# RWKV bonus of a hybrid decoder: two multiplications moved to GpSimd, VectorE's sum placed behind its mix

## The chip, the cores and the metric

The kernel runs on one core of a Trainium2 chip, in one launch. The metric is the device time of the whole program in microseconds (us), lower is better; a figure for the kernel is the median of several executions. PE is TensorE, DVE is VectorE, ACT is ScalarE, POOL is GpSimd, SP is SyncE, which issues most transfers.

## The reference, cut to what matters

One step of a decoder with two layers. Each layer projects its input once and splits the result among three branches: an RG-LRU, an RWKV-7 time mixing with 4 heads of 64, and a latent attention over a paged cache. The three results are gated, joined, projected and normalised. This case concerns the RWKV branch. Its rows are 1040 prompt tokens and 8 sequences of 8 new tokens; here is the part that counts:

```python
u_prev = jnp.concatenate([shift_prev[:, None, :].astype(u.dtype), u[:, :-1]], axis=1)
du = u_prev - u
mix = lp['rk_mix']
xr = u + du * mix[0]
xk = u + du * mix[2]
xv = u + du * mix[3]
r = xr @ lp['rk_wr']
...
k_mod = k.astype(F32) * (1.0 + (a - 1.0) * lp['rk_ka'].astype(F32))
...
o = o + jnp.sum(r_h * k_h * lp['rk_rk'].astype(F32), axis=-1, keepdims=True) * v_h
```

The last line is the bonus: for each token and head, the product of r, the modified key and a weight, summed over the head's 64 elements, times v. All arithmetic is float32.

## The kernel before, in words

Each layer is five blocks with a barrier between them: projection, RWKV, prompt attention, sample attention, output. The RWKV block works on 9 tiles of 128 tokens (RT), t = 0 to 8; in the last one the 64 new tokens sit in the lower half. The first tile's projections, mix and decayed keys are made at the end of the projection block already, beside TensorE's large products; so is the mix of tile 1.

For each tile the block solves a small triangular system, in nine stages by the names prod, n2, z1, z2, z3, mid, zf, wu, wt (SOLVE). This is a chain: TensorE multiplies 32x32 pieces, ScalarE or VectorE takes the result out of PSUM, VectorE transposes or adds, TensorE goes on. Beside each stage the engines do other work on neighbouring tiles, written down in the table BESIDE: for a stage, (work, distance in tiles, piece). From it comes one list, RWKV_ORDER. Every engine walks through the same list and runs the pieces it has a function for (run), so the table sets each engine's order, and semaphores alone tie the engines together. At the stage wt of tile t there stand `("bonus", 1, 0)`, the bonus of tile t + 1, and `("mix", 2, 0)`, the mix of tile t + 2. Before the first tile the list FRONT runs flip and bonus of tile 0.

The pieces that matter, by VectorE's lines in this kernel:
- unit and keys_decay (L1419 to L1437): the last of the new keys. The product L1434 releases s_keys and writes btkt, L1437 writes bk. Both read bbkm, whose half bbkm[:, 1] is the modified key.
- write (L1534, two instructions): updates the running state from PSUM.
- bonus_: rk = r times modified key (L1440), rk = rk times weight (L1441), sums by head into sc4 (L1444), which releases s_bon.
- mix: du (L1386) and six scalar_tensor_tensor (L1391), which release s_mix.
- prod: masks the two PSUM banks of TensorE's stage prod (L1454, L1459), then a transpose and an add (L1463, L1464).

On TensorE, prod (L1064) follows the transposes of flip (L1052), which wait for s_keys, and ScalarE's copy of them (L1291). After prod come low, one read (L1170, L1173) and the first projection of the next tile (L1019). That projection waits for the mix (s_mix) and for VectorE's mask L1459 (s_x), and the stage n2 of the solve stands behind it in TensorE's order. ScalarE, after the copies of flip, scales v by the sums (bonus_, L1298, waits s_bon), then takes out low (L1247, L1248) and the projection (L1255).

GpSimd has little to do in this block: a power of a 128x4 tile twice a tile, as tensor_tensor with ALU.pow (L973 for the key norms, L977 for the group norm), and in the last tile a memset and a product (L982, L990).

Of the kernel before, what the change touches and what calls it, by code (L numbers as in the profile page):

```python
# [18 lines left out]
ALU = mybir.AluOpType  # L19
# [246 lines left out]
def project_block(nc, m):  # L266
# [488 lines left out]
    "mid": [("write", -1, 2), ("gate", -2, 0)],  # L755
    "zf": [("read", -1, 3), ("unit", 1, 0), ("keys_decay", 1, 0)],
    "wu": [("write", -1, 3), ("out", -1, 0), ("flip", 1, 0)],
    "wt": [("bonus", 1, 0), ("mix", 2, 0)]}
FRONT = [("flip", 0), ("bonus", 0)]
RWKV_ORDER = [(f, 0, k) for f, k in FRONT]  # L760
BACK = [("read", 1, 0), ("norm", 0, 0), ("read", 1, 1), ("centre", 0, 0), ("out", 1, 0), ("finish", 0, 0),
# [8 lines left out]
def rwkv_weights(m):  # L770

    w = Memory()
    w.rkw, w.w1, w.w2 = carve(m.work[:, X_AT + DK * T:], (2, 3, WA), (2, 2 * LORA), (2, WA))
    w.prow, w.s_in = carve(m.work[:, W_AT[1] + 8 * Z_COLS - 8 * Z_AT[Z_LOADS[-2]]:W_AT[0]], (7, WA), (NB, 2, HD))
    return w
# [16 lines left out]
def rwkv_block(nc, m):  # L792
# [5 lines left out]
    sem, layer, const = m.sem, m.layer, m.const  # L798
# [8 lines left out]
    s_rkve = sem("s_rkve")  # L807
# [9 lines left out]
    s_keys = sem("s_keys")  # L817
# [3 lines left out]
    s_bon = sem("s_bon")  # L821
# [23 lines left out]
    s_dve = sem("s_dve2")  # L845
    s_sto = sem("s_sto2")
    s_pl = sem("s_pl")
    s_um = sem("s_um")
    rw = rwkv_weights(m)
    rkw, w1, w2, prow, s_in = rw.rkw, rw.w1, rw.w2, rw.prow, rw.s_in  # L850
    fw = rwkv_front(m)
    wl, xm, tw, r_sb, k_sb, v_sb, wa, sg, logd, dec, kk, sqj, ss, bbkm, na, btkt, rt, pc, bk, du = \
# [42 lines left out]
    def heads(x):  # L895
        return x.rearrange("p (h j) -> p h j", h=H_B)
# [12 lines left out]
    def prm(n):  # L909
        return prow[:, n, :]  # L910
# [21 lines left out]
    def steps_to(t):  # L932
        return sum(len(steps(i)) for i in range(t))
# [9 lines left out]
    def of_each(x):  # L943
        return x.rearrange("p (o n) -> p o n", o=1).to_broadcast([NS, SEQ_CH, WA])

    def run(stages):

        for stage, t, k in RWKV_ORDER:
            if stage in stages:
                stages[stage](t, k)  # L950

    N_LD = 16 * 6
    with nc.Block() as block:
        @block.sync
        def _(sp):
            pw = prompt_weights(m)
            for k in range(2):
                sp.dma_start(pw.wuq[:, k], m.wuq[layer, :, k].rearrange("p (h n) -> p h n", h=H_C)).then_inc(m.s_wq, 16)
            sp.dma_start(pw.wuk, m.wuk[layer]).then_inc(m.s_wk, 16)
            sp.dma_start(pw.wuv, m.wuv[layer]).then_inc(m.s_wuv, 16)  # L960
            sp.dma_start(tail, m.consts[:, C_N:]).then_inc(m.s_wuv, 16)
            sp.wait_ge(s_state, steps_to(RT) + 1)
            sp.dma_start(m.o_wkv[layer], s_out).then_inc(s_sto, 16)

            sp.wait_ge(s_sto, 16)

        @block.gpsimd
        def _(pool):
            half = const[:, C_EPS + 1:C_EPS + 2].to_broadcast([P, H_B])

            def keys_norm(t, _):
                pool.wait_ge(s_ss, t + 1)
                nc.gpsimd.tensor_tensor(ss[:, 1, :], ss[:, 0, :], half, ALU.pow).then_inc(s_rn, 1)  # L973

            def norm(t, _):
                pool.wait_ge(s_var, t + 1)
                nc.gpsimd.tensor_tensor(mv[:, :, 3], mv[:, :, 2], half, ALU.pow).then_inc(s_gr, 1)  # L977

            def clear(t, _):
                if t == LAST_T:  # L980
                    pool.wait_ge(s_rkv, 3 * RT)
                    nc.gpsimd.memset(flat_m, 0.0).then_inc(s_pl, 1)  # L982
                    pool.wait_ge(s_pl, 1)

            def split_values(t, _):
                if t == LAST_T:
                    pool.wait_ge(m.s_wuv, 32)
                    pool.wait_ge(s_rkve, 3 * RT)
                    pool.wait_ge(s_rd, 2 * steps_to(LAST_T))
                    nc.gpsimd.tensor_tensor(vm[SMP], of_each(v_sb[SMP, t % 3, :]), own_rows, ALU.mult).then_inc(s_pl, 1)  # L990
                    pool.wait_ge(s_pl, 2)

            run({"keys_norm": keys_norm, "norm": norm, "sums": clear, "wt": split_values})

        @block.tensor
        def _(pe):
            bank = m.bank

            def low(t, _):
                pe.wait_ge(s_fold, 1)  # L1000
                if t >= 1:
                    pe.wait_ge(s_fle, 2 * t)
                for n in range(2):
                    for k in range(2):
                        last = nc.tensor.matmul(bank[7][0:2 * LORA, 0:P], wl[:, n, k, :],
                                                prev_of(t, k) if n else m.ub[:, k, 1 + t * P:1 + (t + 1) * P],
                                                start=n == 0 and k == 0, stop=n == 1 and k == 1)
                last.then_inc(s_lo1, 1)
# [13 lines left out]
            def lora(t, _):  # L1022
                pe.wait_ge(s_lo1e, t + 1)
                for i in range(2):
                    last = nc.tensor.matmul(bank[7][:, i * WA:(i + 1) * WA], tw[0:LORA + 1, i, :], w2[0:LORA + 1, i, :],
                                            start=True, stop=True)
                last.then_inc(s_lo2, 1)

            def sums(t, _):
                pe.wait_ge(s_sg, t + 1)  # L1030
                pe.wait_ge(s_rkve, 3 * t + 3)

                if t == LAST_T:
                    pe.wait_ge(m.s_wuv, 32)
                for i, c in enumerate(sums_of(t)):
                    nc.tensor.matmul(bank[2 + i // 2][:, (i % 2) * WA:(i % 2 + 1) * WA], c, logd,
                                     start=True, stop=True)

                each = tail[:, L_TOT:L_N] if t == LAST_T else sqc(C_B32)[:, 0:P:CH]
                n = 1 + NB if t == LAST_T else C4  # L1040
                for k in range(2):
                    last = nc.tensor.matmul(bank[3][:, WA + n * k:WA + n * k + n], logd[:, k * P:(k + 1) * P],
                                            each, start=True, stop=True)
                last.then_inc(s_cum, 1)
# [314 lines left out]
        def _(dve):  # L1359
# [3 lines left out]
            def link(ins):  # L1363

                chain[0] += 1
                ins.then_inc(s_dve, 1)
                dve.wait_ge(s_dve, chain[0])
# [69 lines left out]
                nc.vector.tensor_tensor(bk[:, t % 3], bbkm, twice(dec[:, 3]), ALU.mult).then_inc(s_hat, 1)  # L1437

            def bonus_(t, _):
                link(nc.vector.tensor_tensor(rk, r_sb, bbkm[:, 1], ALU.mult))  # L1440
                link(nc.vector.tensor_tensor(rk, rk, prm(4), ALU.mult))  # L1441
                if t >= 1:
                    dve.wait_ge(s_bv, t)
                nc.vector.tensor_reduce(sc4, heads(rk), AX, ALU.add).then_inc(s_bon, 1)  # L1444
# [118 lines left out]
            def gate(t, _):  # L1563
                dve.wait_ge(s_of, t + 1)
                for k in range(2):
# [10 lines left out]
            nc.vector.tensor_copy(gnb, bank[4][:, 0:2 * P:P])  # L1576
            run({"mix": mix, "decay": decay, "keys_norm": keys_norm, "unit": unit, "keys_decay": keys_decay,
                 "bonus": bonus_, "prod": prod, "n2": squares, "z1": z1, "z2": z2, "z3": z3, "zf": zf, "read": read,
                 "write": write, "norm": norm, "centre": centre, "finish": finish, "gate": gate})

# [938 lines left out]


BLOCKS = [project_block, rwkv_block, prompt_block, sample_block, output_block]


# [101 lines left out]
```

## Time and profile before

| | us |
|---|---|
| median of 3 runs | 2117.56 |
| lowest and highest | 2106.84, 2118.98 |
| profiled execution, its own time | 2116.25 |
| span of its trace | 2114.5 |
| PE busy in the span | 1966.7 (93%) |
| DVE busy | 1027.3 (49%) |
| ACT busy | 646.4 (31%) |
| POOL busy | 223.1 (11%) |
| RWKV block of layer 0 | about 279 to 490 |
| RWKV block of layer 1 | about 1340 to 1550 |

The trace gives for each engine the instructions in order of time. A start is in us from the span's beginning; what stands in square brackets behind a row is how long the engine had been idle and which instruction's end released it. Equal instructions in a row are merged, with a count. Instructions of VectorE overlap a little: the next starts some 0.08 us before the end of the one ahead unless it waits for it. A matmul's end is modelled.

### The profile page before, as it was taken

To read this page: it belongs to the slowest core of one execution; us is meant where nothing else is said; L and a number is where in the kernel's file an instruction comes from. 1 tells how busy PE (TensorE), PEld (TensorE's weight loads), DVE (VectorE), ACT (ScalarE), POOL (GpSimd) and SP (SyncE) were. 2 spreads that over 40 slices of the span, in tenths; PEclk is the share of its full clock that TensorE was granted. 3 is DMA by queue.
4 is the path that set the end of the run, shared out by engine and by line. 5 is a ranking of instruction groups with operands and counts; after the bars stand their busy time and mean duration, and the time that the engine had idled before them with its cause. 6 is when DMAs were issued, how large, how long until landed. Compare 5 with 4: busy or idle time off the path is not lost. (4 is left out here: it accounts for less than half of the span.)

```text
span 2114.5 us, 51148 instructions
## 1 busy us (share of the span) xinstructions
PE 1966.7 (93%) x22506; PEld 1272.1 (60%) x22506; DVE 1027.3 (49%) x2393; ACT 646.4 (31%) x1719; POOL 223.1 (11%) x223
## 2 busy tenths in 40 slices
PE   8999989988899999999989999899888999999997
PEld 5665667774566567654456656677745665677543
DVE  2017137764565458723330171377745664588333
ACT  1222234442554432210012221344434553323100
POOL 0000000110000034202100000011100000342022
PEclk9999999998999989999999999999989999899999
DMA  5102010000001267721121020100000002577221
GB/s 209 50 1 89 1 48 4 4 4 22 1 1 24 67 232 272 258 110 60 66 62 50 1 89 1 47 4 4 4 22 1 1 13 78 222 271 262 73 80 53
DMA packets 50113, 151.14 MB, mean 71 GB/s; under 512 B 15138, under 2 KB 19490, under 8 KB 40420
## 3 DMA queue, kind: packets, MB, share of 16 engines
q1 hardware_dynamic: 37604, 72.36, 10.3%
q0 software_dynamic: 12288, 75.51, 9.6%
q8 instruction: 179, 2.93, 0.6%
q14 instruction: 42, 0.34, 0.1%
HBM read 130.27 MB, written 12.86 MB: 68 GB/s over the span
## 5 line engine op out<-in xcount | busy, mean ns | idle before, releaser
L405 PE MATMUL psum<-work 128*128 128x368 f32 x1536 | 485.7, 477 | 8.8 <-DMA work<-w_z 6.5
L405 PEld LDWEIGHTS psum<-work 128*128 128x128 f32 x1536 | 294.0, 192 | 194.3 <-issue 9.3
L2458 PE MATMUL psum<-work,mixed 128*128 128x512 f32 (+1 forms) x576 | 250.6, 596 | 1.6 <-PEq L2130 1.6
L2458 PEld LDWEIGHTS psum<-work,mixed 128*128 128x128 f32 (+1 forms) x576 | 106.9, 187 | 138.8 <-issue 138.8
L2326 DVE STREAM_TRANSPOSE work<-work 128x1024 f32<-128x1024 f32 x128 | 150.5, 1214 | 0.7 <-issue 0.5
L1902 ACT ACTIVATE work<-psum,work 128x128 f32<-128x128 f32 (+8 forms) x130 | 97.9, 753 | 162.0 <-DVE work L2005 161.5
L1786 PE MATMUL psum<-work 96*128 96x512 f32 (+3 forms) x384 | 140.0, 499 | 3.7 <-ACT work L1902 2.1
L2070 POOL DMA_INDIRECT work<-cache_ckv,pages x64 | 60.7, 948 | 640.1 <-PE psum L1736 397.4
L2230 PE MATMUL psum<-work,ckv 128*64 128x256 f32 x1024 | 118.4, 382 | 1.9 <-issue 1.2
L1786 PEld LDWEIGHTS psum<-work 96*128 96x128 f32 x384 | 68.3, 192 | 62.5 <-issue 46.0
L2506 DVE SCALAR_TENSOR_TENSOR work<-work,psum 128x512 f32<-128x512 f32 (+1 forms) x36 | 23.1, 684 | 163.9 <-PE psum L2458 163.9
L2004 DVE TENSOR_REDUCE work<-psum 128x1 f32<-128x128 f32 (+8 forms) x130 | 99.5, 765 | 4.4
L2230 PEld LDWEIGHTS psum<-work,ckv 128*64 128x64 f32 x1024 | 73.6, 137 | 42.9 <-issue 13.0
L650 DVE TENSOR_TENSOR mixed<-work 128x1104 f32<-128x1104 f32 x4 | 5.2, 1309 | 193.6 <-ACT work L578 193.5
L1797 PE MATMUL psum<-const_sb,work 128*128 128x128 f32 x594 | 88.7, 285 | 10.1 <-ACT work L1911 9.9
L1911 ACT COPY work<-psum 128x512 f32<-128x512 f32 (+1 forms) x166 | 84.3, 545 | 34.3 <-PE psum L1797 33.6
L1797 PEld LDWEIGHTS psum<-const_sb,work 128*128 128x128 f32 x594 | 69.7, 145 | 37.7 <-issue 19.6
L1729 PE MATMUL psum<-cq,work 128*128 128x368 f32 x192 | 74.3, 520 | 19.1 <-DVE work L1960 16.9
L2003 DVE TENSOR_TENSOR psum<-psum,const_sb 128x128 f32<-128x128 f32 (+1 forms) x130 | 38.2, 294 | 101.5 <-PE psum L1786 87.0
L1815 PE MATMUL psum<-work 128*64 128x128 f32 x1152 | 82.7, 282 | 0.0
L2275 ACT ACTIVATE work<-psum,work 128x1024 f32<-128x1024 f32 x32 | 35.7, 1115 | 132.0 <-DVE work L2337 132.0
L522 ACT ACTIVATE mixed<-psum 128x368 f32<-128x368 f32 x48 | 19.4, 477 | 184.9 <-PE psum L405 184.9
(314 smaller groups left out, 2988.2 us busy)
## 6 DMA issues: line engine op xcount, KB each, us to landing
work<-w_z SPq DMA_DIRECT2D x4, 2560.0 KB, 11.2
work<-w_out SPq DMA_DIRECT2D x4, 2048.0 KB, 9.0
xres<-work SPq DMA_DIRECT2D x16, 512.0 KB, 2.9
work<-xT SPq DMA_DIRECT2D x4, 1104.0 KB, 8.9
work<-x_tok SPq DMA_DIRECT2D x8, 512.0 KB, 3.9
work<-xres SPq DMA_DIRECT2D x8, 512.0 KB, 4.3
work<-w_z SPq DMA_DIRECT2D x1, 2304.0 KB, 12.5
o_ckv<-ckv SPq DMA_DIRECT2D x2, 1104.0 KB, 4.3
```

The costliest lines, as they stand in the source:

```text
L405: return nc.tensor.matmul(zb[i % 2][n][:, 0:G], z_weights(m, g)[:, k, lo:lo + Z_W[i]], xT[:, k, span(n)], start=k == 0, stop=k == DK - 1)
L1729: last = nc.tensor.matmul(bank_of(j)[:, 0:G], wuq[:, k, h, :], cq[:, k, span(g)], start=k == 0, stop=k == 1)
L1786: last = nc.tensor.matmul(m.bank[2 * u + b][:, 0:w], qt[0:96, p % 2, u, t * P:(t + 1) * P], kt[0:96, p % 2, u, a:a + w], start=True, stop= ...
L1797: last = nc.tensor.transpose(m.bank[4 + at % 2][0:w, n * P:(n + 1) * P], pr[:, i % 2, u * N_FULL * P + c * P:u * N_FULL * P + c * P + w], ...
L1815: last = nc.tensor.matmul(m.bank[6][u * VD:(u + 1) * VD, 0:P], val[:, c, (2 * p + u) * VD:(2 * p + u + 1) * VD], pT[:, i % 2, n * P:(n + 1 ...
L1902: nc.scalar.activation(pr[:, i % 2, u * N_FULL * P:u * N_FULL * P + keys(i)], scores_of(i, u), ACT.Exp, bias=mx[:, 2 * (i % 2) + u:2 * (i ...
L1911: nc.scalar.copy(pT[0:w, i % 2, 4 * g * P:(4 * g + len(c)) * P], m.bank[4 + at % 2][0:w, 0:len(c) * P]).then_inc(s_pte, 1)
L2004: link(nc.vector.tensor_reduce(sm, scores_of(i, u), AX, ALU.max))
L2070: pool.indirect_dma_start(rows[n % RING][:, s, :], None, m.cache_ckv, row).then_inc(m.s_pg[n % RING], 16)
L2230: last = nc.tensor.matmul(m.bank[6 + n % 2][64 * s:64 * s + 64, 0:R], pT[:, n % 2, j, 64 * s:64 * s + 64], pgc[n % RING][:, s, j * R:(j + ...
L2326: last = nc.vector.transpose(kt[:, half, s], pgc[n % RING][:, s, :].rearrange("p (j k n) -> p j k n", j=KEYS, k=2) [:, :, half, :])
L2458: last = nc.tensor.matmul(yb[t % 2][half][0:n, :], m.mixed[:, k, lo:lo + n], wo[half][:, k, :], start=k == 0, stop=k == DK - 1)
```

## The change

The two multiplications of the bonus leave VectorE. GpSimd gets a function bonus_ that waits for s_keys (the modified keys), for r (s_rkve) and for the previous tile's sums (s_bon), multiplies r by the key, waits for that on its new semaphore s_rk, and multiplies by the weight. VectorE's bonus_ waits for both on s_rk and does the sums. In the table, mix stands ahead of bonus at the stage wt; that moves the sums behind the mix on VectorE, for every tile that has one. ScalarE's scaling of v stays where it was, as it has no mix. FRONT is as it was, so tile 0's products run on GpSimd too.

```diff
-    "wt": [("bonus", 1, 0), ("mix", 2, 0)]}
+    "wt": [("mix", 2, 0), ("bonus", 1, 0)]}
...
+    s_rk = sem("s_rk")
...
-            run({"keys_norm": keys_norm, "norm": norm, "sums": clear, "wt": split_values})
+            def bonus_(t, _):
+                pool.wait_ge(s_keys, t + 1)
+                pool.wait_ge(s_rkve, 3 * t + 2)
+                if t >= 1:
+                    pool.wait_ge(s_bon, t)
+                nc.gpsimd.tensor_tensor(rk, r_sb, bbkm[:, 1], ALU.mult).then_inc(s_rk, 1)
+                pool.wait_ge(s_rk, 2 * t + 1)
+                nc.gpsimd.tensor_tensor(rk, rk, prm(4), ALU.mult).then_inc(s_rk, 1)
+
+            run({"keys_norm": keys_norm, "norm": norm, "sums": clear, "wt": split_values, "bonus": bonus_})
...
             def bonus_(t, _):
-                link(nc.vector.tensor_tensor(rk, r_sb, bbkm[:, 1], ALU.mult))
-                link(nc.vector.tensor_tensor(rk, rk, prm(4), ALU.mult))
+                dve.wait_ge(s_rk, 2 * t + 2)
                 if t >= 1:
                     dve.wait_ge(s_bv, t)
                 nc.vector.tensor_reduce(sc4, heads(rk), AX, ALU.add).then_inc(s_bon, 1)
```

VectorE's queue at the end of a tile, in the middle of the block, before the change. From the last keys (L1434, L1437) over the state update (L1534) and the bonus to the mix and the masks; the names in brackets are the semaphores waited for, s_pe_prod being TensorE's stage prod:

```order
L1434 TENSOR_TENSOR work<-work 128x512 [waits s_dve2]
L1437 TENSOR_TENSOR work<-work 128x512 [waits s_wr]
L1534 SCALAR_TENSOR_TENSOR work<-work,psum 128x64 [waits s_wr]
L1534 SCALAR_TENSOR_TENSOR work<-work,psum 128x64
L1440 TENSOR_TENSOR work<-work 128x256
L1441 TENSOR_TENSOR work<-work 128x256 [waits s_dve2]
L1444 TENSOR_REDUCE work<-work 128x4 [waits s_bv,s_dve2]
L1386 TENSOR_TENSOR work<-ub 128x256
L1391 SCALAR_TENSOR_TENSOR work<-work,pfs,ub 128x128 [waits s_rkv,s_dve2]
L1391 SCALAR_TENSOR_TENSOR work<-work,pfs,ub 128x128 x5
L1454 TENSOR_TENSOR work<-psum,const_sb 128x512 [waits s_o2,s_pe_prod]
```

The same place in the changed kernel, whose line numbers here are larger by ten and, behind GpSimd's new function and the shorter bonus_, by nine:

```order
L1444 TENSOR_TENSOR work<-work 128x512 [waits s_dve2]
L1447 TENSOR_TENSOR work<-work 128x512 [waits s_wr]
L1543 SCALAR_TENSOR_TENSOR work<-work,psum 128x64 [waits s_wr]
L1543 SCALAR_TENSOR_TENSOR work<-work,psum 128x64
L1396 TENSOR_TENSOR work<-ub 128x256
L1401 SCALAR_TENSOR_TENSOR work<-work,pfs,ub 128x128 [waits s_rkv,s_dve2]
L1401 SCALAR_TENSOR_TENSOR work<-work,pfs,ub 128x128 x5
L1453 TENSOR_REDUCE work<-work 128x4 [waits s_bv,s_rk]
L1463 TENSOR_TENSOR work<-psum,const_sb 128x512 [waits s_o2,s_pe_prod]
```

Two rows are gone, the six products and du have moved up to the state update, and the sums stand directly ahead of the mask, with a wait for GpSimd.

GpSimd's queue in the changed kernel, over two tiles in the middle of the block (L974 and L978 are the powers, L973 and L977 before):

```order
L974 TENSOR_TENSOR work<-work,const_sb 128x4 [waits s_ss]
L999 TENSOR_TENSOR work<-work 128x256 [waits s_bon,s_rkve,s_keys]
L1001 TENSOR_TENSOR work<-work 128x256 [waits s_rk]
L978 TENSOR_TENSOR work<-work,const_sb 128x4 [waits s_var2]
L974 TENSOR_TENSOR work<-work,const_sb 128x4 [waits s_ss]
```

The two products are new between the power for the key norm and the one for the group norm; the other three rows stood there one behind the other.

## Rows read from the trace of the kernel before

**Rows 1.** Windows: us, busy us of each engine, PE clock, DMA share, GB/s.
```profile
core 0: us, PE busy (x) PEld busy (x) DVE busy (x) ACT busy (x) POOL busy (x), PEclk, DMA share, GB/s
...
345.00:367.00 22.00, 20.21 (x640) 16.33 (x623) 16.69 (x60) 10.62 (x38) 2.18 (x2) 1.00 0.02 4
```

**Rows 2.** Timeline, DVE, end of a tile: start, us, engine line operation.
```profile
363.79 0.69 DVE L1434 TENSOR_TENSOR work<-work 128x512 f32<-128x512 f32 x1
364.39 0.69 DVE L1437 TENSOR_TENSOR work<-work 128x512 f32<-128x512 f32 x1
365.11 0.47 DVE L1534 SCALAR_TENSOR_TENSOR work<-work,psum 128x64 f32<-128x64 f32 x2
365.50 0.42 DVE L1440 TENSOR_TENSOR work<-work 128x256 f32<-128x256 f32 x1
365.95 0.42 DVE L1441 TENSOR_TENSOR work<-work 128x256 f32<-128x256 f32 x1
366.41 0.42 DVE L1444 TENSOR_REDUCE work<-work 128x4 f32<-128x256 f32 x1
366.75 0.42 DVE L1386 TENSOR_TENSOR work<-ub 128x256 f32<-128x256 f32 x1
367.20 1.67 DVE L1391 SCALAR_TENSOR_TENSOR work<-work,pfs,ub 128x128 f32<-128x128 f32 x6
368.78 0.69 DVE L1454 TENSOR_TENSOR work<-psum,const_sb 128x512 f32<-128x512 f32 x1
```

**Rows 3.** Timeline, PE, the same place: stage prod, the read, the projection.
```profile
366.35 0.86 PE L1064 MATMUL psum<-work 64*32 64x64 f32 x64 [0.51 <-ACT work L1291]
...
368.52 0.30 PE L1173 MATMUL psum<-work 64*32 64x64 f32 x4
369.81 1.10 PE L1019 MATMUL psum<-work 128*128 128x256 f32 x4 [0.99 <-DVE work L1459]
```

**Rows 4.** Line L1454, whole run: both forms, and whom the engine sat idle for.
```profile
L1454 DVE TENSOR_TENSOR work<-psum,const_sb x16: 681/685/693, 282.6 to 1497.3; 128x512 f32<-128x512 f32 x16
L1454 DVE TENSOR_TENSOR work<-psum,work x2: 692/692/692, 457.1 to 1518.4; 128x512 f32<-128x512 f32 x2
...
  PE psum L1064: 3.4, 4
```

**Rows 5.** Timeline, tile 1 of layer 0: PE's stage prod and the mask.
```profile
301.06 1.06 PE L1064 MATMUL psum<-work 64*32 64x64 f32 x64 [0.25 <-ACT work L1291]
...
302.17 0.69 DVE L1454 TENSOR_TENSOR work<-psum,const_sb 128x512 f32<-128x512 f32 x1
```

**Rows 6.** Groups of GpSimd, forms apart: count, busy us, mean ns, idle before.
```profile
L2482 POOL TENSOR_TENSOR work<-work 128x1024 f32<-128x1024 f32 x16 | 37.5, 2343 | 35.0 <-DVE work L2518 35.0
L973 POOL TENSOR_TENSOR work<-work,const_sb 128x4 f32<-128x4 f32 x16 | 18.6, 1160 | 239.3 <-DVE work L1412 239.3
L977 POOL TENSOR_TENSOR work<-work,const_sb 128x4 f32<-128x4 f32 x18 | 18.2, 1009 | 163.8 <-DVE work L1548 163.8
L2479 POOL TENSOR_TENSOR work<-work,const_sb 128x1 f32<-128x1 f32 x16 | 8.8, 553 | 249.0 <-DVE work L2514 249.0
...
L389 POOL COPY ub<-work 128x8 f32<-128x8 f32 x4 | 0.8, 196 | 0.1
```

**Rows 7.** Timeline, where GpSimd's powers meet VectorE's instructions.
```profile
248.72 0.42 DVE L730 SCALAR_TENSOR_TENSOR work<-work 128x256 f32<-128x256 f32 x1
248.96 1.08 POOL L397 TENSOR_TENSOR work<-work,const_sb 128x4 f32<-128x4 f32 x1 [104.24 <-DVE work L729]
...
360.13 0.43 DVE L1414 SCALAR_TENSOR_TENSOR work<-work 128x256 f32<-128x256 f32 x1
360.26 1.17 POOL L973 TENSOR_TENSOR work<-work,const_sb 128x4 f32<-128x4 f32 x1 [9.71 <-DVE work L1412]
360.59 0.47 DVE L1534 SCALAR_TENSOR_TENSOR work<-work,psum 128x64 f32<-128x64 f32 x2
```

**Rows 8.** Timeline, ACT, the same place as rows 2.
```profile
366.87 1.07 ACT L1298 ACTIVATE work<-work 128x64 f32<-128x64 f32 x4 [0.29 <-DVE work L1444]
...
368.55 0.26 ACT L1248 COPY work<-psum 32x128 f32<-32x128 f32 x1
370.95 0.48 ACT L1255 ACTIVATE work<-psum,const_sb 128x256 f32<-128x256 f32 x1 [2.15 <-PE psum L1019]
```

## The prediction, made before the changed kernel was run

> **What bounds the kernel now.** The change touches the RWKV block alone, so I read the windows of that block first. A tile takes 22 us, in which PE is busy for 20.2, DVE for 16.7, ACT for 10.6 and POOL for 2.2, at a granted clock of 1.00, the 2.4 GHz level [rows 1]. PE's share says little: the block is a chain that goes back and forth between engines. What counts is where PE stands still. The largest such place is the first projection of the next tile (L1019): PE's read ends at 368.52 + 0.30 = 368.82, the projection starts at 369.81, and the 0.99 us between are put down to DVE's mask L1459 [rows 3]. The n2 stage of the solve stands behind that projection, so the whole chain waits.
>
> Why is the mask late? DVE's timeline shows it. PE's stage prod, which the mask reads, ends at 366.35 + 0.86 = 367.21 [rows 3], and L1454 starts at 368.78, with no idle time ahead of it: DVE is still in the bonus and the mix [rows 2]. So for 1.57 us DVE's queue is what the chain waits for. Over the run 18 such masks stand, and only 4 of them found DVE idle, 3.4 us together [rows 4]: tiles 0 and 8 of each layer, which have no mix ahead. The other 14 (tiles 1 to 7, two layers) are held by the queue. In tile 1 PE's prod ends at 301.06 + 1.06 = 302.12 and the mask starts at 302.17 [rows 5], so there nearly nothing is to be had.
>
> **What is removed.** L1440 starts at 365.50 and L1444 at 366.41 [rows 2]: the two products and their waits take 0.91 us of DVE's queue. PE can use all of it, since its gap is 0.99. In 12 tiles (2 to 7, twice) a mask 0.91 us earlier makes the chain 0.91 us shorter. The end of the mask's wait for prod would be 1.57 away, so it isn't reached.
>
> **What is added.** GpSimd gets two products of 128x256. No row has that form. Its 128x1024 add takes 2.34 us; a copy of 128x8, nearly all fixed cost, 0.196; a power of one element per partition 0.55 [rows 6]. Bounds: a pure share of the large one, 2.34 / 4 = 0.585; and with the fixed cost of the power, 0.55 + (2.34 - 0.55) / 4 = 1.00. With the copy's fixed cost it is 0.19 + (2.34 - 0.19) / 4 = 0.73, which I take as D, because a product has no power's work in it.
>
> If nothing came in between, GpSimd would start some 0.08 after L1434's end at 363.79 + 0.69 = 364.48 and end both by 366.1, even with D at 1.00 by 366.7. DVE asks for them behind the mix, at 367.5. So the wait on s_rk would cost nothing; the cover is the mix (1.67 us) and the state update (0.47).
>
> **But the two engines seem to exclude each other.** The power takes 1.01 us at L977 and 1.16 at L973, the same operation and size [rows 6]. At L973 it begins at 360.26 while DVE's L1414, with two SBUF tensors as inputs, runs until 360.13 + 0.43 = 360.56: 0.30 of overlap, 0.16 longer. At L397 the overlap is 248.72 + 0.42 - 248.96 = 0.18, and the power takes 1.08, 0.07 longer [rows 7]. Both fit: GpSimd's reading waits until about 0.14 before the reported end of DVE's instruction. DVE's L1534, one input in SBUF and one in PSUM, takes its usual 0.47 beside the running power [rows 2, 7]. So an instruction of DVE with two SBUF inputs holds GpSimd off. The other direction, GpSimd holding DVE off, no row shows. Its bounds are 0 and the whole of each product; I take the whole, as a shared path that excludes one way most likely does so the other way too.
>
> The Trainium skill says this in "SBUF — State Buffer", section "Who interferes with whom": a VectorE instruction with two SBUF inputs contends with a GpSimd instruction that reads SBUF, and whoever comes first holds the path for its whole instruction. For GpSimd's waiting the trace agrees, with 0.16 and 0.07 us; by a rule without it the sum would be the first rival's. Its "GPSIMD Engine Reference", section 3.1, gives 4497 ns for a two-input add of 2048 elements; an estimate from that and our 2343 ns for 1024 is 2.10 ns an element and 0.73 us for 256, against 0.73 from the rows.
>
> **The sum with exclusion.** Taken on the tile of rows 2.
> - The first product is asked for at 364.56, L1437 (two SBUF inputs) runs until 365.08. It ends at 365.08 - 0.14 + D = 364.94 + D.
> - L1534 runs beside it. L1386 (du, both inputs in SBUF) could start at 365.50, where L1440 stood. It is held until the product ends: D - 0.56 = 0.17 us.
> - The second product is asked for at 365.75, while L1386 runs for its 0.42 us. DVE's next, L1391, waits for L1386's end, so GpSimd is in line first. It ends at L1386's end - 0.14 + D. L1391 would have started 0.03 after L1386's end (366.75 + 0.42 to 367.20): held for D - 0.17 = 0.56 us.
> - The six products of the mix and the sums then run as before, only in another order (1.58 and 0.34 between starts).
>
> The hold is 2D - 0.73 = 0.73 us against 0.91 removed: 0.18 us gained a tile, 12 x 0.18 = 2.2 us. In tile 1 of each layer there is no state update to cover the first product, so about 0.5 us more is held, and the tile loses 0.3: 0.6 for both. Tiles 0 and 8 have no mix: DVE waits out both products, some 0.1 us longer than its own took, which goes into the idle time ahead of the mask (3.4 us over four). Net gain 1.5 us. Against the profiled execution's own 2116.25 (2114.5 of span and 1.75 around it) that is 2114.7; the median of the runs shown is 1.3 higher, the lowest run 9.4 lower. I say 2115.
>
> **What could be late next.** The sums now end 1.2 us later, and ACT's L1298 waits for them, with low (until L1248) and the projection's L1255 queued behind it. From the mask's start: the sums end 0.08 after it, then 0.05, 1.07 for L1298 and 0.55 for low, so ACT is free at 1.75; L1255 was needed at 370.95 - 368.78 = 2.17 [rows 2, 8]. 0.42 us of cover are left, and they move with the mask, so this costs nothing. On POOL's queue the group norm's power stands behind the products; it is wanted only after prod's masks, so it isn't late. PE's order is unchanged.
>
> **The rivals.**
> - GpSimd doesn't hold DVE off. For it: the rows show only the opposite direction. Then 12 x 0.91 = 10.9 us come off, in tile 1 between 0 and 0.9 more: about 11, 2105.
> - The products together cost DVE more than it gave up. Held time is 2D - 0.73, removed 0.91, so it decides at D = 0.82. With D = 1.00 it loses 0.36 a tile and about 0.86 in each tile 1: 4.3 + 1.7 = 6.0, 2122.3. For it: GpSimd's fixed costs are uncertain, and each handing over may cost something I took as nothing. Against it: 0.585 as a lower bound, by which 0.47 a tile or 5.6 us come off, 2110.6.
> - DVE's mix gets ahead of the second product, which then runs behind it: last product of the mix at 365.67 + 0.42 + 0.03 + 1.67 = 367.79, the product until 368.38, the sums at 368.43, the mask at 368.77 against 368.78. The same time as before, 2116, and DVE seen waiting on s_rk.
>
> **How the numbers follow.** Exclusion with a net within 4 us of nothing (my sum, or the mix ahead): 0.55. No hold on DVE, around 2105: 0.17. GpSimd dearer, 2119 to 2122: 0.23. Something else, a changed clock or a run's spread beyond these: 0.05. The range takes in the outer two: 2103 to 2123. The likeliest case's own range is 2111 to 2118. About 1%, 21 us, is what a measurement of this kernel can tell from no change, and no case here reaches it: same 0.94, faster 0.04, slower 0.02.
>
> **What would show it.** If I am right, the timeline shows GpSimd's first product longer than its second's plain time or starting under L1437, L1386's and L1391's counterparts late or long, and PE's gap ahead of the projection still 0.7 to 0.9 us, a tile of about 21.9. If DVE isn't held, the gap falls to about 0.1 and the tile takes 21.1. If GpSimd is dearer, its products take over 0.82 us and the gap grows. I would be wrong altogether if the mask found DVE idle, if ACT's L1255 counterpart were late, or if the time moved in a block other than RWKV.

## The result and the profile after

The changed kernel takes 2107.73 us in the median (2097.22 to 2118.56), before 2114.73 (2106.84 to 2121.15), 20 runs each: a ratio of 0.9965, 95% interval 0.9952 to 0.9979. That is 7 us less, where 2115 was forecast. The interval stands for 4.4 to 10.2 us. The time lies inside the range of 2103 to 2123, but below the likeliest case's own 2111 to 2118.

DVE and POOL at the end of a tile in the changed kernel, from the last keys (L1444, L1447) to the mask (L1463); L999 and L1001 are GpSimd's two products, L1396 is du, L1401 the mix, L1453 the sums:

```profile
361.33 0.69 DVE L1444 TENSOR_TENSOR work<-work 128x512 f32<-128x512 f32 x1
361.93 0.69 DVE L1447 TENSOR_TENSOR work<-work 128x512 f32<-128x512 f32 x1
362.09 1.12 POOL L999 TENSOR_TENSOR work<-work 128x256 f32<-128x256 f32 x1 [3.13 <-DVE work L1444]
362.65 0.47 DVE L1543 SCALAR_TENSOR_TENSOR work<-work,psum 128x64 f32<-128x64 f32 x2
363.04 0.45 DVE L1396 TENSOR_TENSOR work<-ub 128x256 f32<-128x256 f32 x1
363.29 0.70 POOL L1001 TENSOR_TENSOR work<-work 128x256 f32<-128x256 f32 x1
363.52 1.93 DVE L1401 SCALAR_TENSOR_TENSOR work<-work,pfs,ub 128x128 f32<-128x128 f32 x6
365.37 0.41 DVE L1453 TENSOR_REDUCE work<-work 128x4 f32<-128x256 f32 x1
365.70 0.68 DVE L1463 TENSOR_TENSOR work<-psum,const_sb 128x512 f32<-128x512 f32 x1
...
387.12 0.67 DVE L1463 TENSOR_TENSOR work<-psum,const_sb 128x512 f32<-128x512 f32 x1
```

From bk's start (L1447) to the mask it is 3.77 us, where it was 368.78 - 364.39 = 4.39 [rows 2]: 0.62 us less. The next mask comes 21.42 us later; a tile took 22.04 us before (its masks at 346.74 and 368.78). Those are the quickest tiles, which I compare throughout; others take up to 22.93 before and 22.24 after, at the same granted clock of 1.00, and why is open. Both engines' marks are there: GpSimd's first product takes 1.12 us, and on VectorE du takes 0.45 for 0.42 and the mix 1.93 for 1.67 [rows 2]. That is 0.29 us of the 0.91 given back.

TensorE at the same place, its read and the projection behind it:

```profile
366.06 0.30 PE L1183 MATMUL psum<-work 64*32 64x64 f32 x4
366.72 1.10 PE L1029 MATMUL psum<-work 128*128 128x256 f32 x4 [0.36 <-DVE work L1468]
```

The gap ahead of the projection has gone from 0.99 [rows 3] to 0.36 us. So 0.62 a tile in 12 tiles is 7.4 us, and the medians show 7.0, with the interval above.

The profiled execution's span is 14.6 us shorter, 2099.9 for 2114.5, and that must not be read as the change's gain. From the first mask to the last it is 5.0 us in layer 0's block (174.50 to 169.49) and 2.7 in layer 1's (175.33 to 172.67). The stretch between the blocks, which the change doesn't touch, is 9.5 us longer in before's execution (885.95 to 876.45 from layer 0's last mask to layer 1's first), and over the experiments below it goes from 879.3 to 886.6. The granted clock goes with it: 0.96 over the 885.95 us and 0.97 over the 876.45, and in the experiments 0.96 over the longest, 886.55, and 0.97 over the shortest, 879.32. 1.27 us of layer 1's gain are missing in its first stretch, from the mask of tile 0 to that of tile 1, which took 20.70 us at a granted clock of 0.84, and 19.43 at 0.91 before. A trace shows the mechanism here, and the medians show the sum.

### The profile page after: what moved, and what is told of

The parts are those of the page before. It is cut to its first block and busy times, and to the rows that moved or that the text cites. A ratio compares the mean times of both kernels' runs of the same rounds, so it can differ in the third digit from the quotient of the medians.

```text
span 2099.9 us, 51166 instructions
## 1 busy us (share of the span) xinstructions
PE 1957.1 (93%) x22506; PEld 1264.7 (60%) x22506; DVE 1017.3 (48%) x2357; ACT 644.5 (31%) x1719; POOL 254.7 (12%) x259
## 5 line engine op out<-in xcount | busy, mean ns | idle before, releaser
L1085 PE MATMUL psum<-work 32*32 32x32 f32 x4608 | 63.2, 197 | 14.0 <-DVE work L1476 5.8
```

Source lines behind the costliest of these rows:

```text
L1085: last = nc.tensor.matmul(bank_[rows(c), g * CH:(g + 1) * CH], lhs[rows(c), g, 0:CH], rhs[rows(c), g, 0:CH], start=True, stop=True)
```

## The experiments

Each is compared at the same place: from bk's start to the mask, and from one mask to the next, in the quickest tiles in the middle of layer 0's block. Line numbers move a little with the edits.

**The order alone.** Both products stay on VectorE.

```diff
-    "wt": [("bonus", 1, 0), ("mix", 2, 0)]}
+    "wt": [("mix", 2, 0), ("bonus", 1, 0)]}
```

> Only the table is changed: mix ahead of bonus, both products still on VectorE. My theory (the gain comes from taking the two products off VectorE's queue, less what GpSimd's instructions hold it up): the same instructions stand ahead of the mask, so from the start of bk's product (L1437) to the mask it stays 4.39 us, a tile stays at 22.04 us, and the time is that of before within 0.1%. ScalarE's scaling comes 1.2 us later and is covered by 0.42. Rival (the new order is what helps, because du and the mix start earlier): a tile falls below 22 us, up to the 21.42 of the changed kernel.

```profile
347.61 0.68 DVE L1454 TENSOR_TENSOR work<-psum,const_sb 128x512 f32<-128x512 f32 x1
...
365.26 0.68 DVE L1437 TENSOR_TENSOR work<-work 128x512 f32<-128x512 f32 x1
...
369.64 0.68 DVE L1454 TENSOR_TENSOR work<-psum,const_sb 128x512 f32<-128x512 f32 x1
369.76 1.06 ACT L1298 ACTIVATE work<-work 128x64 f32<-128x64 f32 x4 [2.32 <-DVE work L1444]
...
371.81 0.47 ACT L1255 ACTIVATE work<-psum,const_sb 128x256 f32<-128x256 f32 x1 [0.56 <-PE psum L1019]
```

Those rows are DVE's masks and bk's product, and ACT's scaling and projection. 4.38 us and 22.03 a tile: no gain. The time is 2113.55 against 2115.34, a ratio of 0.999 (0.9977 to 1.0003). ScalarE's scaling comes late, as foreseen, and the projection's copy still finds it idle, 0.56 us before. The order by itself is worth nothing.

**GpSimd alone.** The changed kernel with the table of before, so that the sums and the mix wait for GpSimd.

```diff
-    "wt": [("mix", 2, 0), ("bonus", 1, 0)]}
+    "wt": [("bonus", 1, 0), ("mix", 2, 0)]}
```

> Only the engine is changed: both products on GpSimd, the table as before, so VectorE's sums and the mix behind them wait for GpSimd's second product. My theory: counted from bk's start the first product ends at 1.28 us (0.68 - 0.14 + 0.73), the second at 2.00, the sums start at 2.05, the mask at 4.42 against 4.39 before: a tile of 22.07 us, VectorE idle about 0.5 us ahead of the sums, the time that of before within 0.1%. Rival (the order has nothing to do with it): 21.42 us a tile as in the changed kernel.

```profile
364.49 0.68 DVE L1447 TENSOR_TENSOR work<-work 128x512 f32<-128x512 f32 x1
364.65 1.12 POOL L999 TENSOR_TENSOR work<-work 128x256 f32<-128x256 f32 x1 [3.12 <-DVE work L1444]
...
365.85 0.64 POOL L1001 TENSOR_TENSOR work<-work 128x256 f32<-128x256 f32 x1
366.52 0.42 DVE L1453 TENSOR_REDUCE work<-work 128x4 f32<-128x256 f32 x1 [0.84 <-POOL work L1001]
366.85 0.42 DVE L1396 TENSOR_TENSOR work<-ub 128x256 f32<-128x256 f32 x1
...
367.31 1.67 DVE L1401 SCALAR_TENSOR_TENSOR work<-work,pfs,ub 128x128 f32<-128x128 f32 x6
368.89 0.68 DVE L1463 TENSOR_TENSOR work<-psum,const_sb 128x512 f32<-128x512 f32 x1
```

The rows are DVE's and POOL's at the end of a tile. The mask comes 4.40 us after bk's start, a tile takes 22.05, and the time is 2116.81 against 2115.34, a ratio of 1.000 (0.9983 to 1.0017). VectorE's idle time before the sums is 0.84, which the expectation had at 0.5, though the sums start at 2.03, where it said 2.05. Here du and the mix run when GpSimd is done, and take their plain 0.42 and 1.67. The engine alone is worth nothing either: the change pays only with both its halves, the products off VectorE and the mix as cover for GpSimd's slower ones.

**The products left out.** What the change would bring if GpSimd cost nothing. No engine multiplies, the sums are taken over r alone, so the bonus is wrong, and the mix stands ahead of them as in the changed kernel.

```diff
-    "wt": [("bonus", 1, 0), ("mix", 2, 0)]}
+    "wt": [("mix", 2, 0), ("bonus", 1, 0)]}
...
             def bonus_(t, _):
-                link(nc.vector.tensor_tensor(rk, r_sb, bbkm[:, 1], ALU.mult))
-                link(nc.vector.tensor_tensor(rk, rk, prm(4), ALU.mult))
...
-                nc.vector.tensor_reduce(sc4, heads(rk), AX, ALU.add).then_inc(s_bon, 1)
+                nc.vector.tensor_reduce(sc4, heads(r_sb), AX, ALU.add).then_inc(s_bon, 1)
```

> The two products are left out on every engine (the sums are taken over r instead), the mix stands ahead of the sums: what the change would give if GpSimd cost nothing. My theory: the mask starts 0.91 us earlier than before, 3.48 us after bk's start, a tile takes 21.13 us, PE's gap ahead of the projection is about 0.1 us; 11 us off the whole, a ratio of about 0.995; so 0.29 us a tile of the changed kernel is what GpSimd holds up. Rival (the chain limits the gain, not GpSimd): 21.42 us a tile here too.

```profile
362.19 0.68 DVE L1437 TENSOR_TENSOR work<-work 128x512 f32<-128x512 f32 x1
...
363.74 1.67 DVE L1391 SCALAR_TENSOR_TENSOR work<-work,pfs,ub 128x128 f32<-128x128 f32 x6
...
365.66 0.68 DVE L1452 TENSOR_TENSOR work<-psum,const_sb 128x512 f32<-128x512 f32 x1
```

3.47 us to the mask and 21.11 to 21.12 a tile, 0.92 less than before; 2103.00 against 2115.34, a ratio of 0.9957 (0.9935 to 0.998). So the chain can take the whole 0.91, and the changed kernel's 0.30 a tile above this is GpSimd's price.

**GpSimd writing only, and GpSimd reading one operand.** What of GpSimd's work is it that costs VectorE time? Both with the waits and signals of the changed kernel, and with the sums over r, so the bonus is wrong here too. In the code scr is memory that nothing else uses, and some stands for the parameter rows.

```diff
...
-                nc.gpsimd.tensor_tensor(rk, r_sb, bbkm[:, 1], ALU.mult).then_inc(s_rk, 1)
+                nc.gpsimd.memset(scr[:, 0:720], 0.0).then_inc(s_rk, 1)
                 pool.wait_ge(s_rk, 2 * t + 1)
-                nc.gpsimd.tensor_tensor(rk, rk, prm(4), ALU.mult).then_inc(s_rk, 1)
+                nc.gpsimd.memset(scr[:, 0:720], 0.0).then_inc(s_rk, 1)
...
-                nc.vector.tensor_reduce(sc4, heads(rk), AX, ALU.add).then_inc(s_bon, 1)
+                nc.vector.tensor_reduce(sc4, heads(r_sb), AX, ALU.add).then_inc(s_bon, 1)
```

> As the changed kernel, but GpSimd's two products are replaced by two memsets of 128x720 into unused memory, about 0.70 us each, with the same waits and signals; VectorE's sums are taken over r. GpSimd writes and reads nothing. Theory A (GpSimd's reading is what holds VectorE): du takes its 0.42 us and the six products of the mix 1.67, a tile 21.12 us as with the products left out. Theory B (any GpSimd work of that length holds VectorE, or the signals and waits do): du 0.45, the mix about 1.9, a tile of 21.4 us.

DVE and POOL with the memsets, which run beside bk's product, du and the mix:

```profile
341.62 0.68 DVE L1448 TENSOR_TENSOR work<-work 128x512 f32<-128x512 f32 x1
...
342.73 0.42 DVE L1397 TENSOR_TENSOR work<-ub 128x256 f32<-128x256 f32 x1
343.18 1.67 DVE L1402 SCALAR_TENSOR_TENSOR work<-work,pfs,ub 128x128 f32<-128x128 f32 x6
...
345.09 0.68 DVE L1464 TENSOR_TENSOR work<-psum,const_sb 128x512 f32<-128x512 f32 x1
```

```profile
341.76 0.70 POOL L1000 MEMSET work<- 128x720 f32 x1 [3.10 <-DVE work L1445]
342.52 0.70 POOL L1002 MEMSET work<- 128x720 f32 x1
```

Neither engine is lengthened, and the masks follow each other by 21.11 to 21.12 us, as with nothing on GpSimd. Now the same with copies, set against the run with memsets:

```diff
...
-                nc.gpsimd.memset(scr[:, 0:720], 0.0).then_inc(s_rk, 1)
+                nc.gpsimd.tensor_copy(scr[:, 0:600], some[:, 0:600]).then_inc(s_rk, 1)
                 pool.wait_ge(s_rk, 2 * t + 1)
-                nc.gpsimd.memset(scr[:, 0:720], 0.0).then_inc(s_rk, 1)
+                nc.gpsimd.tensor_copy(scr[:, 0:600], some[:, 0:600]).then_inc(s_rk, 1)
```

> As the run with memsets, but with two GpSimd copies of 128x600 from the parameter rows into unused memory, about 0.68 us each, so it reads one operand. Theory A (reading is what holds VectorE): L999's place is lengthened by bk's product to over 1 us, du is held a little (0.45 or more), the first product of the mix goes to about 0.6, a tile of 21.4 us as in the changed kernel. Theory B (it takes two operands on GpSimd): 21.12 us a tile.

```profile
341.69 1.08 POOL L1001 COPY work<-work 128x600 f32<-128x600 f32 x1 [3.11 <-DVE work L1446]
342.83 0.78 POOL L1003 COPY work<-work 128x600 f32<-128x600 f32 x1
```

```profile
341.54 0.69 DVE L1449 TENSOR_TENSOR work<-work 128x512 f32<-128x512 f32 x1
...
342.65 0.42 DVE L1398 TENSOR_TENSOR work<-ub 128x256 f32<-128x256 f32 x1
343.10 1.97 DVE L1403 SCALAR_TENSOR_TENSOR work<-work,pfs,ub 128x128 f32<-128x128 f32 x6
...
345.32 0.68 DVE L1465 TENSOR_TENSOR work<-psum,const_sb 128x512 f32<-128x512 f32 x1
```

The first copy is held by bk's product to 1.08 us, the second holds the mix for 0.30, and a tile takes 21.41 to 21.42 us, as with the products. I had expected a small hold on du too; there is none, since the first copy lets go in time. It is GpSimd's reading of SBUF that VectorE waits for, with one operand as with two, and neither its writing nor the semaphores. Each of these two ran once, 2102.97 us with memsets and 2105.73 with copies, beside 2116.85 for the median of before, so their verdict is the trace's.

**A third product.** Into unused memory, and nobody waits for it.

```diff
...
-                pool.wait_ge(s_rk, 2 * t + 1)
+                pool.wait_ge(s_rk, 3 * t + 1)
                 nc.gpsimd.tensor_tensor(rk, rk, prm(4), ALU.mult).then_inc(s_rk, 1)
+                pool.wait_ge(s_rk, 3 * t + 2)
+                nc.gpsimd.tensor_tensor(scr[:, 0:WA], prm(4), prm(5), ALU.mult).then_inc(s_rk, 1)
...
-                dve.wait_ge(s_rk, 2 * t + 2)
+                dve.wait_ge(s_rk, 3 * t + 2)
```

> The changed kernel with a third GpSimd product of 128x256 (two parameter rows into unused memory) behind the second; VectorE doesn't wait for it. It is asked for while the mix's products run back to back on VectorE with no wait between them. If GpSimd gets in at the next end of a VectorE instruction, one more product of the mix is held for 0.4 to 0.5 us, the mask comes that much later, a tile of 21.9 us. If it has to wait until VectorE has a wait of its own or an instruction that doesn't read two tensors, it takes over 1.5 us and the tile stays at 21.42. If GpSimd doesn't hold VectorE at all, the tile stays and the product takes 0.64.

```profile
346.28 0.73 POOL L1004 TENSOR_TENSOR work<-work 128x256 f32<-128x256 f32 x1
```

```profile
345.74 2.47 DVE L1404 SCALAR_TENSOR_TENSOR work<-work,pfs,ub 128x128 f32<-128x128 f32 x6
...
348.46 0.67 DVE L1466 TENSOR_TENSOR work<-psum,const_sb 128x512 f32<-128x512 f32 x1
```

The third product takes the 0.73 us of an undisturbed one although VectorE's six products follow each other without a wait: GpSimd gets in between two of them. The mix goes from 1.93 to 2.47, bk's start to the mask from 3.77 to 4.32 us, and the next masks come after 21.96 to 22.21 us. Against the 4.39 and 22.04 of before 0.07 us of the gain are left, for an instruction that no one waits for. Its one run took 2119.03 us, where before's took 2109.78 to 2120.81.

**One product early.** r times the weight as soon as r is there, at the stage n2, so that only the product with the key is left behind the keys.

```diff
-    "n2": [("proj", 1, 1), ("lora", 1, 0), ("write", -1, 0)],
+    "n2": [("proj", 1, 1), ("weigh", 1, 0), ("lora", 1, 0), ("write", -1, 0)],
...
-FRONT = [("flip", 0), ("bonus", 0)]
+FRONT = [("weigh", 0), ("flip", 0), ("bonus", 0)]
...
             def bonus_(t, _):
                 pool.wait_ge(s_keys, t + 1)
+                pool.wait_ge(s_rk, 2 * t + 1)
+                nc.gpsimd.tensor_tensor(rk, rk, bbkm[:, 1], ALU.mult).then_inc(s_rk, 1)
+
+            def weigh(t, _):
                 pool.wait_ge(s_rkve, 3 * t + 2)
                 if t >= 1:
                     pool.wait_ge(s_bon, t)
-                nc.gpsimd.tensor_tensor(rk, r_sb, bbkm[:, 1], ALU.mult).then_inc(s_rk, 1)
-                pool.wait_ge(s_rk, 2 * t + 1)
-                nc.gpsimd.tensor_tensor(rk, rk, prm(4), ALU.mult).then_inc(s_rk, 1)
+                nc.gpsimd.tensor_tensor(rk, r_sb, prm(4), ALU.mult).then_inc(s_rk, 1)
...
```

> The changed kernel with its first product made another way: r times the weight on GpSimd as soon as r is there (stage n2, where VectorE is idle for 2.6 us), so that behind the keys only one product is left, with the modified key. My theory: the second hold (0.26 us on the mix) goes, the first (0.03 on du) stays: the mask comes 3.51 us after bk's start, a tile takes 21.15 us, about 3.5 us off against the changed kernel and 10.5 off against before, a ratio of 0.995. Rival (the mix is slower for another reason than GpSimd's second product): 21.42 us as in the changed kernel.

```profile
345.43 1.02 POOL L997 TENSOR_TENSOR work<-work 128x256 f32<-128x256 f32 x1 [3.12 <-DVE work L1446]
```

```profile
345.27 0.68 DVE L1449 TENSOR_TENSOR work<-work 128x512 f32<-128x512 f32 x1
...
346.38 0.42 DVE L1398 TENSOR_TENSOR work<-ub 128x256 f32<-128x256 f32 x1
346.83 1.67 DVE L1403 SCALAR_TENSOR_TENSOR work<-work,pfs,ub 128x128 f32<-128x128 f32 x6
...
348.74 0.68 DVE L1465 TENSOR_TENSOR work<-psum,const_sb 128x512 f32<-128x512 f32 x1
```

The one product is still held by bk's, holds nothing itself here, and the mask comes after 3.47 us, a tile of 21.11 to 21.12: all of GpSimd's price is gone in these tiles. I had left 0.03 us for du; but this product writes over one of its inputs and takes 0.64 where nothing holds it, and so lets go 0.1 us sooner. In tile 1 of each layer, where no state update stands between, it does hold du, which takes 0.87 and 0.86. The time is 2105.29 against 2116.85, a ratio of 0.9951 (0.9936 to 0.9966).

**All on VectorE, where it is idle.** The product with the weight when r comes, and the product with the key and the sums one tile later, both at the stage n2, where VectorE waits 2.6 us for the state update. ScalarE's scaling goes to z1. GpSimd has nothing new to do.

```diff
-    "n2": [("proj", 1, 1), ("lora", 1, 0), ("write", -1, 0)],
-    "z1": [("read", -1, 1), ("proj", 1, 2), ("decay", 1, 0), ("centre", -2, 0)],
+    "n2": [("bonus", 0, 0), ("proj", 1, 1), ("weigh", 1, 0), ("lora", 1, 0), ("write", -1, 0)],
+    "z1": [("scale", 0, 0), ("read", -1, 1), ("proj", 1, 2), ("decay", 1, 0), ("centre", -2, 0)],
...
-    "wt": [("bonus", 1, 0), ("mix", 2, 0)]}
-FRONT = [("flip", 0), ("bonus", 0)]
+    "wt": [("mix", 2, 0)]}
+FRONT = [("flip", 0), ("weigh", 0)]
...
                 if t >= 1 and n < 2:
-                    act.wait_ge(s_bon, t)
+                    act.wait_ge(s_keys, t)
...
-            run({"low": low, "proj": proj, "lora": lora, "sums": sums, "flip": flip, "bonus": bonus_, "n2": squares,
+            run({"low": low, "proj": proj, "lora": lora, "sums": sums, "flip": flip, "scale": bonus_, "n2": squares,
...
             def bonus_(t, _):
-                link(nc.vector.tensor_tensor(rk, r_sb, bbkm[:, 1], ALU.mult))
-                link(nc.vector.tensor_tensor(rk, rk, prm(4), ALU.mult))
+                link(nc.vector.tensor_tensor(rk, rk, bbkm[:, 1], ALU.mult))
...
+            def weigh(t, _):
+                dve.wait_ge(s_rkve, 3 * t + 2)
+                if t >= 1:
+                    dve.wait_ge(s_bon, t)
+                link(nc.vector.tensor_tensor(rk, r_sb, prm(4), ALU.mult))
...
```

> All of the bonus on VectorE, but in another place: r times the weight as soon as r is there, and the product with the key and the sums one tile later, both at the stage n2, where VectorE sits idle for 2.6 us ahead of the state update; ScalarE's scaling at the stage z1. GpSimd does nothing new. My theory: 1.25 us leave the stretch ahead of the mask (two products 0.91, the sums 0.34), the gain is capped by PE's gap of 0.99 us, so a tile of about 21.05 us, 12 to 14 us off the whole, a ratio near 0.994. Rival (the chain through n2 and z1 has no room for three more instructions): VectorE's transposes or the state update come late, and a tile stays above 21.4 us.

It took 2101.21 us against 2115.34, a ratio of 0.9924 (0.989 to 0.9957). To set it beside the changed kernel, both were run again on one chip:

> The changed kernel as it is, on the same chip and against the same runs of before as the next one. My theory: 7 us below before, a ratio of 0.9965, tiles of 21.42 us.

> The version with all of the bonus on VectorE in its idle time once more, on the same chip as the changed kernel. My theory: tiles of 21.04 us in the middle of the block against 22.04 of before and 21.42 of the changed kernel, so 12 to 14 us below before and 5 to 7 below the changed kernel, a ratio of 0.9935 to 0.9945. Rival (the earlier timing was a lucky one, tiles 1 and 8 give back what the middle ones gain): no better than the changed kernel, 0.9965.

The changed kernel took 2107.34 us (ratio to before 0.9952, 0.9932 to 0.9971) and this one 2103.91 (0.9937, 0.9916 to 0.9957), before 2116.83. From the trace of its second run, DVE's and PE's rows at the mask, and DVE's at n2: L1440 is the product with the key, L1443 the sums, L1449 the product with the weight for the next tile, L1539 the state update:

```profile
365.59 0.68 DVE L1459 TENSOR_TENSOR work<-psum,const_sb 128x512 f32<-128x512 f32 x1
...
366.58 0.30 PE L1173 MATMUL psum<-work 64*32 64x64 f32 x4
...
366.81 1.13 PE L1019 MATMUL psum<-work 128*128 128x256 f32 x4
...
368.93 0.38 DVE L1440 TENSOR_TENSOR work<-work 128x256 f32<-128x256 f32 x1
369.35 0.42 DVE L1443 TENSOR_REDUCE work<-work 128x4 f32<-128x256 f32 x1
...
370.32 0.43 DVE L1449 TENSOR_TENSOR work<-work 128x256 f32<-128x256 f32 x1 [0.55 <-ACT work L1258]
371.69 0.47 DVE L1539 SCALAR_TENSOR_TENSOR work<-work,psum 128x64 f32<-128x64 f32 x2 [0.95 <-PE psum L1208]
```

PE's gap ahead of the projection is gone (no idle time is noted there), the three instructions sit in idle time, since VectorE still waits 0.95 us for the state update, and the next mask comes 21.03 us later (at 386.62), 1.01 less than before. The gain is capped by PE, as expected: 1.25 us were taken out ahead of the mask. Most tiles took longer than that, 21.1 to 21.5 us in this run. In one that took 21.39 in both runs (from the mask at 344.20 in this one) the update at n2 came late, with 1.31 us of idle time ahead of it for 0.95; what delayed it is open. From the mask of tile 1 to that of tile 8 its two traces show 149.3 and 148.7 us in layer 0 and 151.1 and 148.9 in layer 1, the changed kernel's two 149.7 and 150.9, and 152.0 and 153.3, and before's 154.9 and 155.9. So it is the fastest of the versions that compute the whole bonus, in the medians and in the block; between its total and the changed kernel's the intervals overlap, so on the whole program that order is likely and not shown.

## Why the prediction was partly right, and which term was off

The forecast was 1.5 us off the whole, and 7.0 were measured. That the time still lies in the range is owed to the range's width, which took in the times of the rivals. The mechanism of my case was there, and one term of its sum was far too large.

- **The bound.** Right. DVE's queue ahead of the mask held the chain, 0.91 us were to be had (0.92 with the products left out), and PE's gap shrank with it.
- **The cover.** Right. The sums never waited for GpSimd where a mix stood ahead of them (4 waits in all, 3.5 us, at tiles 0 and 8), and in those the mask still waited for PE. With the cover gone, in the second experiment, the gain was gone.
- **The first product.** D = 0.73 is what GpSimd's first product takes where nothing holds it (0.74 at 278.76 in tile 0), and it ended 1.28 us after bk's start: 361.93 + 1.28 = 363.21, as 362.09 + 1.12 gives. The step on GpSimd's waiting, until 0.14 before DVE's reported end, held to 0.01 us.
- **The exclusion.** Right for these products, in both directions. That GpSimd holds VectorE too was an assumption, for which I had no row; the lengthened du and mix show it, and the runs of memsets and copies show that it is the reading. By "SBUF — State Buffer" of the Trainium skill, section "Who interferes with whom", VectorE's two-input instructions contend with GpSimd instructions that read SBUF, and not with those that only write; the traces agree on that, with 21.42 us a tile for copies and 21.12 for memsets.
- **The hold's length, the term that failed.** "Its bounds are 0 and the whole of each product; I take the whole." The sum had DVE held to GpSimd's reported end, 0.17 + 0.56 = 0.73 us; measured were 0.03 + 0.26 = 0.29. GpSimd lets go before its reported end. du took 0.03 longer than 0.42, so it was free 0.14 before L999's end. The mix was lengthened by 0.26: its first product, 0.35 long, ended 0.14 after L1001's end at 363.99, so it was free 0.21 before. The second product also takes 0.64 where nothing holds it, and not 0.73. With these, 0.17 - 0.14 = 0.03 and 0.56 - 0.09 - 0.21 = 0.26, and the gain is 0.62 a tile for the forecast 0.18. I had measured the same 0.14 for GpSimd's waiting and left it out for DVE's. The sign of being right that hung on this term failed too: PE's gap was to stay at 0.7 to 0.9 us and a tile at about 21.9, and they came to 0.36 and 21.42, which is nearer to the 0.1 and 21.1 that I gave for no hold at all.
- **A row that I had missed.** "The other direction, GpSimd holding DVE off, no row shows" is not so. In the trace of before, at the end of layer 0's block, a power of GpSimd's runs while VectorE starts two products with both inputs in SBUF (L1521):

```profile
486.46 1.01 POOL L977 TENSOR_TENSOR work<-work,const_sb 128x4 f32<-128x4 f32 x1 [7.11 <-DVE work L1548]
486.67 1.29 DVE L1521 TENSOR_TENSOR work<-work 128x512 f32<-128x512 f32 x2
```

The two take 1.29 us, the plain time of such a pair (L1434 and L1437 start 0.60 apart and take 0.69 [rows 2]), though 0.80 us of the power were still to come. So an instruction of GpSimd that reads SBUF does not hold VectorE for its whole span. That the hold covers only the time in which GpSimd reads, most of a product and little of a power with its four elements, would fit both; no run tests that.
- **Tile 1.** I had it lose 0.3 us a layer for want of cover. du was indeed held for half a us there:

```profile
297.69 0.68 DVE L1447 TENSOR_TENSOR work<-work 128x512 f32<-128x512 f32 x1
...
298.29 0.95 DVE L1396 TENSOR_TENSOR work<-ub 128x256 f32<-128x256 f32 x1
...
301.45 0.67 DVE L1463 TENSOR_TENSOR work<-psum,const_sb 128x512 f32<-128x512 f32 x1
```

That is 3.76 us from bk's start to the mask. Before it was 302.17 - 298.27 = 3.90 [rows 5], with bk's row

```profile
298.27 0.68 DVE L1437 TENSOR_TENSOR work<-work 128x512 f32<-128x512 f32 x1
```

So du's hold of 0.53 and the mix's of 0.25 stayed below the 0.91 removed, and the tile lost nothing.
- **The rivals.** The time fell between my case (within 4 us of nothing) and the first rival, no hold at all, 2105, where I had named no case. That rival is refuted by the lengthened du and mix, and by the copies; its time was near because the hold is short. The dearer GpSimd (D above 0.82) is out, at 0.73 and 0.64. The mix getting ahead of the second product did not happen: even between instructions with no wait GpSimd gets in, as the third product shows.
- **What could be late next.** Right. ScalarE's projection copy found 0.56 us of idle time in the changed kernel (L1265, at 367.86) and as much in the run with the order alone, where I had left it 0.42.

## What to carry to other kernels

Work that moves from VectorE to GpSimd can cost VectorE time where GpSimd reads SBUF when VectorE wants to start an instruction with two SBUF inputs, also if no one waits for it: here a third of what the move took away (0.29 of 0.91 us a tile), and nearly all of it with one product more. Put GpSimd's reading beside instructions that read PSUM or one tensor, or let it end under one that VectorE started first, and for products and copies count the hold to some 0.13 to 0.21 us before GpSimd's reported end. And before another engine is asked, look whether the same engine stands idle elsewhere in the period: three instructions in VectorE's own idle time brought 1.01 us in the quickest tiles, where the other engine brought 0.62.

## What the runs showed of the hardware

- Held instructions are reported as long, not as late: du starts at 298.29 and takes 0.95 us for its usual 0.42. A group's mean shows it, an idle time doesn't.
- VectorE goes on 0.13 to 0.21 us ahead of GpSimd's reported end, in products as in copies (343.61 for the second copy's end, the mix lengthened by 0.30). Beside the power of 128x4 it went on with 0.80 us of 1.01 still to come. "SBUF — State Buffer" of the Trainium skill, section "SBUF: two separate sides", says that the path is held for the whole instruction; by the reported times it is held for less, and the measurement decides.
- Instructions of VectorE with one input in SBUF keep their time beside a product of GpSimd: the state update (L1543, its other input in PSUM) takes 0.47 us beside L999, and the sums take 0.42 beside the third product (tile 0 of that run, at 280.95).
- GpSimd's product of 128x256 takes 0.73 us from two other tensors into a third (0.74, 0.73) and 0.64 where the output is one of the inputs. I had no reason to expect a difference, and why there is one is open.
